# A chunked scan on TensorE: RWKV output products of the old state placed ahead of the state product

## The reference, cut to what matters

```python
def step(s, inp):
    r_t, w_t, k_t, v_t, kk_t, a_t = inp
    sa = jnp.einsum('bhvk,bhk->bhv', s, -kk_t)
    s = (s * w_t[:, :, None, :] + sa[..., None] * (kk_t * a_t)[:, :, None, :]
         + v_t[..., None] * k_t[:, :, None, :])
    return s, jnp.einsum('bhvk,bhk->bhv', s, r_t)
```

## Time and profile before

| | |
|---|---|
| median of 3 runs | 1820.44 us (1815.37 to 1821.44) |
| profiled execution | 1820.15 us, span from first to last instruction 1818.4 us |
| busy share of the span | PE 98%, PEld 81%, DVE 63%, ACT 37%, POOL 32% |
| mean granted clock of TensorE | 0.996 of full speed |
| the scan | 749.5 to 919.6 us, 16 chunks |
| line 1388 | 256 matmul records of 222 ns in the median |
| line 1390 | 256 matmul records of 222 ns in the median |

### The profile page before, as it was taken

The page is one execution under the profiler, slowest core; times in us unless marked ns, Lnnn a source line. Parts: engine busy times, 40 slices in busy tenths (PEclk is TensorE's granted clock), DMA queues, the critical chain, the costliest instruction groups (busy, mean ns, idle before and its releaser), DMA issues.

```text
span 1818.4 us, 28338 instructions
## 1 busy us (share of the span) xinstructions
PE 1782.1 (98%) x11148; PEld 1471.0 (81%) x11148; DVE 1140.8 (63%) x1352; ACT 665.0 (37%) x1126; POOL 588.0 (32%) x420
## 2 busy tenths in 40 slices
PE   8999999999999999999999999999999999999997
PEld 7778788777788888788878778788888888888885
DVE  2856666566419930377768754966666665665577
ACT  3535434235322112355642221343333333444341
POOL 1211222221222332444414542755455554500000
PEclk9999999999999999999999999999999999999999
DMA  6256574325673377487575573225545455489463
GB/s 178 52 111 147 141 183 127 81 76 145 173 192 94 101 169 215 138 250 238 164 240 168 149 230 98 93 70 186 168 133 177 136 177 176 145 281 314 159 230 145
DMA packets 386436, 293.25 MB, mean 161 GB/s; under 512 B 172428, under 2 KB 318412, under 8 KB 384256
## 3 DMA queue, kind: packets, MB, share of 16 engines
q1 hardware_dynamic: 310080, 237.63, 44.1%
q10 hardware_dynamic: 76224, 53.81, 10.4%
HBM read 196.33 MB, written 94.98 MB: 160 GB/s over the span
## 4 chain that ended last, share of the span: by engine, by line
PE 39%; DVE 7%; issue 1%; POOL 1%; DMA 1%; ACT 1%; SPq 0%; DVEq 0%; ACTq 0%
PE b_ps L165 8%; PE b_ps L166 8%; PE b_ps L167 8%; PE f_ps L165 3%; PE f_ps L167 3%; PE f_ps L166 3%; PE b_ps L158 3%; PE b_ps L159 2%; PE b_ps L160 2%; POOL ob_lo L2003 1%; DVE y L2621 1%; DVE y L2481 1%; DMA ff_raw<-in_ffn_down 1%; DVE x1lo L2572 1%; DVE y L2624 0%
## 5 line engine op out<-in xcount | busy, mean ns | idle before, releaser
L158 PE MATMUL bank<-xhi,w_hi 128*128 128x512 f32 x960 | 379.0, 395 | 1.8 <-DVE xlo L989 0.7
L160 PE MATMUL bank<-xhi,w_lo 128*128 128x512 f32 x960 | 374.4, 390 | 0.0
L159 PE MATMUL bank<-xlo,w_hi 128*128 128x512 f32 x960 | 373.8, 389 | 0.0
L461 POOL TENSOR_TENSOR w_lo<-w_raw,w_hi 128x1024 fp32r<-128x1024 f32 x60 | 170.5, 2841 | 546.3 <-ACT w_hi L846 546.3
L158 PEld LDWEIGHTS bank<-xhi,w_hi 128*128 128x128 f32 x960 | 180.2, 188 | 42.5 <-issue 5.0
L160 PEld LDWEIGHTS bank<-xhi,w_lo 128*128 128x128 f32 x960 | 180.2, 188 | 38.4
L159 PEld LDWEIGHTS bank<-xlo,w_hi 128*128 128x128 f32 x960 | 180.4, 188 | 36.3
L2031 POOL TENSOR_TENSOR ff_ring_lo<-ff_w_sums,ff_ring_hi 128x512 fp32r<-128x512 f32 x88 | 125.5, 1427 | 75.5 <-ACT ff_ring_hi L2306 75.4
L2031 POOL TENSOR_TENSOR ff_ring_lo<-ff_raw,ff_ring_hi 128x512 fp32r<-128x512 f32 x66 | 95.8, 1452 | 152.0 <-ACT ff_ring_hi L2306 152.0
L826 ACT ACTIVATE work<-bank 128x512 f32<-128x512 f32 x68 | 40.7, 598 | 244.8 <-PE bank L160 228.9
L165 PE MATMUL b_ps<-x1hi,ff_ring_hi 128*128 128x512 f32 x264 | 103.1, 391 | 0.0
(11 more groups left out here) (416 smaller groups left out, 3971.3 us busy)
## 6 DMA issues: line engine op xcount, KB each, us to landing
w_raw<-in_w_in ACTq DMA_DIRECT2D x61, 512.0 KB, 4.4
hid_ops<-y SPq DMA_DIRECT2D x77, 256.0 KB, 2.9
ff_raw<-hid_ops SPq DMA_DIRECT2D x77, 256.0 KB, 3.9
op<-opnd SPq DMA_DIRECT2D x16, 1152.0 KB, 5.5
u<-work ACTq DMA_DIRECT2D x68, 256.0 KB, 4.0
b_gate<-u SPq DMA_DIRECT2D x24, 512.0 KB, 3.8
ff_raw<-in_ffn_gate SPq DMA_DIRECT2D x22, 512.0 KB, 4.6
ff_raw<-in_ffn_up SPq DMA_DIRECT2D x22, 512.0 KB, 5.9
```

The source lines that it names most:

```text
L158: pe.matmul(out, w_hi, x_hi, start=first, stop=False)
L159: pe.matmul(out, w_hi, x_lo, start=False, stop=False)
L160: return pe.matmul(out, w_lo, x_hi, start=False, stop=last)
L461: pool.tensor_tensor(w_lo[b][:, :, :], w_raw[b][:, :, :], as_f32(w_hi[b][:, :, :]), ALU.subtract).then_inc(w_lo_done, 1)
```

## The change

The 8 products of line 1388 leave `outputs` and become a function of their own, `state_outputs`, which also takes the wait for o_done. It is called ahead of `rwkv_update`, thus between `inverse_first` of the next chunk and the state product. The 8 products with wv (line 1390) stay in `outputs` and add to what is in ps_o already. Since the first 8 products are now issued in one run, only those with j = 0 carry the start flag, one on each half of the partitions; the others write to the same bank without it.

```diff
+            def rwkv(j, e):
+                return ps_o[rwkv_rows(e), j * C:(j + 1) * C]
+
+            def state_outputs(c):
+                d = c % DEEP
+                if c:
+                    pe.wait_ge(o_done, c)
+                for j in range(4):
+                    for e in range(2):
+                        pe.matmul(rwkv(j, e), ar[d][:, 4 * e + j, 1, :], sv[d][:, 4 * e + j, :], start=j == 0, stop=True, skip_group_check=j > 0)
+
             def outputs(c):
                 b, d = c % 2, c % DEEP
                 pe.wait_ge(masked, c * 4 + 4)
-                if c:
-                    pe.wait_ge(o_done, c)
-                rwkv = lambda j, e: ps_o[rwkv_rows(e), j * C:(j + 1) * C]
                 gdn = lambda p, e: ps_o[rwkv_rows(e), 256 + p * GD:256 + (p + 1) * GD]
                 for j in range(4):
                     for e in range(2):
-                        pe.matmul(rwkv(j, e), ar[d][:, 4 * e + j, 1, :], sv[d][:, 4 * e + j, :], start=True, stop=False)
-                    for e in range(2):
-                        pe.matmul(rwkv(j, e), causal[b][:, 4 * e + j, :], wv[d][:, 4 * e + j, :], start=False, stop=True)
+                        pe.matmul(rwkv(j, e), causal[b][:, 4 * e + j, :], wv[d][:, 4 * e + j, :], start=False, stop=True, skip_group_check=True)
...
                 if c == 0:
                     scores(c)
+                state_outputs(c)
                 rwkv_update(c)
                 outputs(c)
                 gdn_update(c)
```

## The result

The changed kernel took 1822.97 us in the median of 22 runs, beside 1820.05 us for the kernel before in as many: ratio 1.0016, 95% interval 1.0009 to 1.0024, which is +1.6 to +4.4 us. One of the 22 runs of the changed kernel took 5434.84 us, a disturbed one; the ratio leaves it out. The profiled execution took 1819.32 us with a span of 1817.5, thus less than the one of before: the total of one execution can't show an effect of this size, but the ordinary chunks inside it can.

The account below looks back on a forecast made before the run. A loop over PE, VectorE and ScalarE (state product, softmax rest, quotients) bounds ordinary chunks, PE's order level with it. Terms: 8 x 0.16 = 1.3, 3 x 0.22 = 0.7, less 0.1 to 0.8: +1.4, 1821.8 us; range 1816.5 to 1826.5.

Parts of the forecast that it names:

- The bound: In an ordinary scan chunk ScalarE's quotients hold the last load of line 1415 by 0.04 us; PE's order ends together.
- The size of the delay: Before line 1365: moved products take 0.46 us, 0.24 fits the wait for wv, so the state product comes 0.22 later.
- The 0.07: After the inverse step: moved products start 0.07 us before the last inverse matmul ends, as at the first chunk's shape change.
- What is given back: At the chunk's head: VectorE's strict masks end earlier, so line 1342 starts 0.06 us sooner; net +0.16 per ordinary chunk.
- The sum: Over the scan's 16 chunks: +1.1 to +1.8 us, taken as +1.4.
- the stops: PE's idle time with nothing to wait for, "issue", in or right behind the output products; 0.82 us at 853.36.
- the three chunks that PE ended: Chunks at 803.0, 814.0 and 845.8, where PE stops and ScalarE is done long before; 0.1 to 0.8 us gained together.
- PE's order is the bound: Rival, chance 0.13: in the scan only the filled wait counts, 14 chunks x 0.24 = 3.4 us gained, 1817.0.
- Nothing fits into the wait: Rival, chance 0.14: before line 1365 the state product is 0.46 us late, and the loop with it; +4.4, 1824.8.
- The stops move: Rival, chance 0.08: one instruction less per chunk shifts PE's causeless stops; all gone 1818.3 us, doubled 1825.3.
- the four long chunks: Four scan chunks of 10.8 to 11.2 us, 0.7 to 1.1 over the ordinary one, 3.5 in all.
- The time: Whole kernel: 1821.8 us against the median 1820.44, a change of 0.08%; within 0.3% given chance 0.81.

Follow-up runs that it names:

- the second: The changed kernel once more, unaltered, beside the kernel before: 1821.51 against 1820.07 us, ratio 1.0007 (0.9998 to 1.0017).

## Why the prediction was right, and where it was not

*The bound.* Right. The loop over the state product, the softmax rest and the quotients ends an ordinary chunk: 10.25 with the products ahead of the state product, 10.02 with half of them, 10.14 with none, and 10.36 against 10.60 when PE is made the bound.

*The size of the delay.* Right: the moved loads start at 872.54, 0.07 before the last inverse matmul ends (871.72 + 0.89), and 0.46 later the state product loads. The 0.07 came from one row of the first chunk and held in each of the 14 chunks between the first and the last.

*What is given back.* Too small: 0.06 was put for line 1342, and it is 0.10. The prediction took the start, 0.49 behind line 1337 in place of 0.55, and that is what came. But the group also runs in 0.64, not 0.69: once the masks are early, its loads run 0.11 ahead of its matmuls (867.68 and 867.79), so that its end comes 0.11 earlier. The loop starts from that end. Hence +0.11 a chunk, where +0.16 was forecast, and 10.25, where 10.3 was.

*The sum.* +1.4 was forecast and +1.31 found in the profiled scan, but part of that agreement is chance. The smaller step of 0.11 counts for 14 chunks in this division, not for 11. The prediction let the stops stay in the three chunks that PE ended and gave these -0.1 to -0.8; but most stops went elsewhere, and the excess fell by 0.18 in all. In the changed kernel the stops of chunks 5 and 9, behind the state product, cost 0.43 and 0.44 less than their length, and three new ones came ahead of it, where they cost 2.6 in full. That the excess hardly moved is luck. The first chunk, put at 0, is +0.06, and the last, put at -0.06, is -0.11.

*The rivals.* "PE's order is the bound" is false here and true once 0.46 us of other work is on PE: then the gain is its 0.24 a chunk. "Nothing fits into the wait" is refuted by the 0.07. "The stops move" happened, to other instructions and mostly to other chunks; it did not shift the sum, 3.68 to 3.50 and 4.12 us. (The 3.5 that the prediction gave to the four long chunks comes from rounded rows; by the starts of the chunks these four hold 3.25, and the others 0.43.)

*The time.* 1821.8 was forecast; 1822.97 and 1821.51 were measured. The effect stayed within 0.3%, which the prediction took for the least that a measurement can tell, from three runs; with 22 runs of each kernel the interval is 0.15% wide, and all of it lies above no change. Why the first comparison gave +2.9 and the second +1.4 isn't settled by the runs: the loop is good for 1.3, and the excess of the middle chunks alone ranged from 2.7 to 4.1 us over five profiles with this loop. That the scatter of the stops makes the difference is thus an inference from their size, not shown run by run. Nor is it the only scatter: in three of the twelve other profiles the granted clock also fell for 3.4 to 6.8 us in the input projection or the feed-forward block, behind waits of PE of 1.9 to 2.7 us, which it did not in those of the kernel before and the changed one.

## What to carry to other kernels

A wait that is filled is a gain only if the engine that waits also ends the stage: here the same move gains 0.24 us a chunk, gains 0.19, or costs 0.11, according to whether PE's order ends the chunk, hands that over to a loop through two other engines, or has been level with it. Fill a wait with no more than fits into it (half of the products: -0.12 a chunk), and put what must be early in a loop ahead of what merely has time. Where a long unrolled program shows idle time put down to "issue", count the engine's instructions before looking for a cause in the work around it.

## What the runs showed of the hardware

- PE's stops over 0.4 us lie at every 256th of its instructions and follow the count when eight or sixteen instructions are added far ahead. They were up to 2.6 us long, differed from execution to execution at the same instruction, and in the changed kernel ended 1.26 to 1.50 us after a 16 KB packet had landed in the queue q8. Of 354 such boundaries 73 showed a stop of 0.2 us or more.
- Work that is put at the end of a phase on an engine that was idle there (GpSimd, 1.3 us, with a wait that held up its later work by 9 us) cost 5 us: PE's next phase stood for 8.71 in place of 2.28 us, and the clock stayed at its lower level for 10.2 and 13.7 us in place of 6.8.
- A change of tile shape from 64*64 to 128*64 lets the next load start 0.07 us before the last matmul ends (an end that is modelled), in each of 14 chunks; where the shape stays, from line 1388 to 1365, it starts 0.23 before.
- VectorE's addition of 128x4 elements took 0.16 us, and 0.39 and 0.61 in the median in the kernels where GpSimd scaled a state beside it.
